# Dividing the 544 tokens of a matmul panel at another column: 272+272, 288+256, 512+32 and 364+180 in the four feed-forward stages of a decoder step

## The reference

```
x = x + 0.5 * swiglu(rms_norm(x, ffn1_norm), w_gate, w_up, w_down)
x = x + mixer(rms_norm(x, mix_norm))
x = x + 0.5 * swiglu(rms_norm(x, ffn2_norm), w_gate, w_up, w_down)
```

## Time and profile before

| what | value |
|---|---|
| time, median of 2 runs | 2168.56 us (2167.45 to 2169.67) |
| profiled execution, first to last instruction (its span) | 2169.2 us |
| PE busy | 2121.6 us, 98% of the span |
| PEld busy | 2040.0 us, 94% |
| DVE busy | 1028.8 us, 47% |
| ACT busy | 690.9 us, 32% |
| POOL busy | 274.7 us, 13% |
| TensorE clock granted, mean | 0.990 of full |
| HBM | 218.65 MB moved, 101 GB/s |

### The profile page before, as it was taken

One profiled execution on the slowest core, in us unless ns is written; L12 is line 12 of the kernel. 1 busy time (PEld: TensorE's weight loads), 2 busy tenths in 40 slices (PEclk: granted clock), 3 DMA queues, 4 the chain that ended last, 5 costly groups with the idle time before them and its releaser, 6 DMA issues.

```text
span 2169.2 us, 41417 instructions
## 1 busy us (share of the span) xinstructions
PE 2121.6 (98%) x16662; PEld 2040.0 (94%) x16662; DVE 1028.8 (47%) x1300; ACT 690.9 (32%) x908; POOL 274.7 (13%) x290
## 2 busy tenths in 40 slices
PE   9999999999999999999999999999988899999997
PEld 8999999997999999999999999999844799999997
DVE  6442444567654324455442444656835364424443
ACT  5221222237254212224441222222334244412221
POOL 0000111300310000021000001403145320000012
PEclk9999999999999999999999999999999999999999
DMA  3222432222132222222222222322589322222221
GB/s 143 87 96 79 131 108 94 91 69 73 69 107 89 91 83 88 89 93 71 86 102 83 78 90 96 112 91 83 153 236 267 117 85 87 102 82 78 87 100 68
DMA packets 68710, 218.65 MB, mean 101 GB/s; under 512 B 10186, under 2 KB 22645, under 8 KB 68544
## 3 DMA queue, kind: packets, MB, share of 16 engines
q1 hardware_dynamic: 58864, 191.00, 26.2%
q0 software_dynamic: 9184, 24.80, 4.1%
q10 hardware_dynamic: 576, 1.67, 0.2%
HBM read 212.67 MB, written 5.78 MB: 101 GB/s over the span
## 4 chain that ended last, share of the span: by engine, by line
PE 92%; DVE 3%; ACT 1%; DMA 1%; issue 1%; SPq 1%; DVEq 0%; ACTq 0%
PE ps L646 87%; PE ps L1067 1%; DVE rinv L1543 1%; DMA keys<-pool_kt 1%; DVE w_lo L1533 1%; PE ps L1094 1%; SPq L523 0%; PE ps L999 0%; ACT prob L1311 0%; DMA x<-xT 0%; PE ps L974 0%; PE ps L665 0%; PE ps L949 0%; PE ps L986 0%; PE ps L960 0%
## 5 line engine op out<-in xcount | busy, mean ns | idle before, releaser
L1210 ACT ACTIVATE w_hi<-raw 128x1024 fp32r<-128x1024 f32 (+2 forms) x298 | 334.8, 1124 | 1181.4 <-PE ps L646 1173.4
L646 PE MATMUL ps<-hx_hi,w_hi 128*128 128x272 f32 x3376 | 702.6, 289 | 5.1 <-DVE w_lo L1533 2.9
L646 PE MATMUL ps<-hx_hi,w_lo 128*128 128x272 f32 x3376 | 699.5, 289 | 0.0
L646 PE MATMUL ps<-hx_lo,w_hi 128*128 128x272 f32 x3376 | 696.9, 288 | 0.0
L646 PEld LDWEIGHTS ps<-hx_hi,w_hi 128*128 128x128 f32 x3376 | 531.8, 188 | 9.9 <-issue 5.8
L646 PEld LDWEIGHTS ps<-hx_lo,w_hi 128*128 128x128 f32 x3376 | 531.5, 189 | 0.0
L646 PEld LDWEIGHTS ps<-hx_hi,w_lo 128*128 128x128 f32 x3376 | 527.8, 189 | 0.0
L1533 DVE TENSOR_TENSOR w_lo<-raw,w_hi 128x1024 fp32r<-128x1024 f32 (+2 forms) x298 | 421.1, 1413 | 97.0 <-ACT w_hi L1210 96.7
L646 PE MATMUL ps<-hid_hi,w_hi 128*128 128x272 f32 x1408 | 291.1, 288 | 0.0
L646 PE MATMUL ps<-hid_lo,w_hi 128*128 128x272 f32 x1408 | 290.9, 288 | 0.0
L646 PE MATMUL ps<-hid_hi,w_lo 128*128 128x272 f32 x1408 | 290.8, 288 | 0.0
(11 more groups left out here) (315 smaller groups left out, 1516.5 us busy)
## 6 DMA issues: line engine op xcount, KB each, us to landing
raw<-gu SPq DMA_DIRECT2D x175, 512.0 KB, 3.2
raw<-down SPq DMA_DIRECT2D x64, 704.0 KB, 4.0
keys<-pool_kt SPq DMA_DIRECT2D x128, 144.0 KB, 4.5
vals<-pool_v POOLq DMA_DIRECT2D x128, 128.0 KB, 4.7
raw<-odd_in SPq DMA_DIRECT2D x21, 512.0 KB, 3.2
raw<-even_in SPq DMA_DIRECT2D x14, 512.0 KB, 3.2
raw<-even_out SPq DMA_DIRECT2D x8, 512.0 KB, 3.2
raw<-odd_out SPq DMA_DIRECT2D x8, 512.0 KB, 3.9
```

Source lines behind the costliest of these rows:

```text
L646: last = pe.matmul(acc[slot][0:m, a, 0:TH], w, r[:, t, a * TH:(a + 1) * TH], start=(begin and t == tiles[0] and one == 0), stop=((end if s ...
L1210: act.activation(w_hi[slot][:, 0:cols], raw[slot][:, 0:cols], ACT.Copy).then_inc(w_hi_done, 1)
```

## The change

The cut column becomes a parameter of the stage. The two matmuls of a product take columns 0 to split - 1 and split to 543. The accumulator is now one run of 544 columns, placed so that its column `split` is the first of the second bank; each matmul still writes in one bank. The stages f0 to f3 get the splits 272, 288, 512 and 364; the mixers keep 272.

```
+SPLIT = 272
+FFN_SPLIT = (272, 288, 512, 364)
...
-        def acc_of(slot, rows=P):
-            return acc[slot][0:rows, :, 0:TH]
+        def acc_of(slot, rows=P, split=SPLIT):
+            at0 = 2 * slot * BANK + BANK - split
+            return ps_flat[rows if isinstance(rows, slice) else slice(0, rows), at0:at0 + T]
...
-                    for w, r, one in ((hi, rhs_hi, 0), (hi, rhs_lo, 1), (lo, rhs_hi, 2)):
-                        for a in token_halves:
-                            last = pe.matmul(acc[slot][0:m, a, 0:TH], w, r[:, t, a * TH:(a + 1) * TH],
...
+                    for a in token_halves:
+                        c0, c1 = (0, split) if a == 0 else (split, T)
+                        out = acc_of(slot, m, split)[:, c0:c1]
+                        pe.matmul(out, hi, rhs[:, 0, t, c0:c1], start=opens, stop=False)
+                    for a in token_halves:
+                        c0, c1 = (0, split) if a == 0 else (split, T)
+                        pe.matmul(acc_of(slot, m, split)[:, c0:c1], hi, rhs[:, 1, t, c0:c1], start=False, stop=False)
+                    for a in token_halves:
+                        c0, c1 = (0, split) if a == 0 else (split, T)
+                        last = pe.matmul(acc_of(slot, m, split)[:, c0:c1], lo, rhs[:, 0, t, c0:c1], start=False, stop=closes)
```

The readers of the accumulator take one run of 544 columns in place of two of 272 (BANK is 512):

```
-                        dve.tensor_tensor(halves(gate[:]), acc_of(n0 % 2), halves(rinv[:]), ALU.mult).then_inc(acc_read, 1)
+                        dve.tensor_tensor(gate[:], acc_of(n0 % 2, split=split), rinv[:], ALU.mult).then_inc(acc_read, 1)
...
-                dve.scalar_tensor_tensor(out=xm, in0=acc_of(slot), scalar=factor, in1=xm, op0=ALU.mult, op1=ALU.add)\
+                dve.scalar_tensor_tensor(out=xm, in0=acc_of(slot, split=split), scalar=factor, in1=xm, op0=ALU.mult, op1=ALU.add)\
```

More of the change, by code:

```diff
@@ L153, in decoder_step @@
         put = region(region_hid, end_hid)
-        mix_hi = put("mix_hi", [P, DT, T], F32R)
-        mix_lo = put("mix_lo", [P, DT, T], F32R)
+        mix = put("mix", [P, 2, DT, T], F32R)
+        mix_hi, mix_lo = mix[:, 0], mix[:, 1]
+        mix_base = [region_hid + s * size([P, DT, T]) for s in range(2)]
         spare = region_hid + 2 * size([P, DT, T])
@@ L288, in decoder_step @@
         ps_flat = ps[:].rearrange("p b c -> p (b c)")
-        acc = [ps[:, 2 * s:2 * s + 2, :] for s in range(2)]
+        BANK = 512
         def sem(name):
@@ L631, in _, with panel @@
         def _(pe):
-            def panel(n, slot, rhs_hi, rhs_lo, tiles, wait_input=None, m=P, begin=True, end=True, token_halves=(0, 1), stop=None, first=False):
+            def panel(n, slot, rhs, tiles, wait_input=None, m=P, begin=True, end=True, token_halves=(0, 1), stop=None, first=False, split=SPLIT):
                 if begin:
@@ L643, in panel @@
                     hi, lo = w_hi[slot][:, t * m:(t + 1) * m], w_lo[slot][:, t * m:(t + 1) * m]
[L644 to L648 removed]
+                    opens = begin and t == tiles[0]
+                    closes = (end if stop is None else stop) and t == tiles[-1]
+                    for a in token_halves:
[8 more added lines that the diff above has]
+                        last = pe.matmul(acc_of(slot, m, split)[:, c0:c1], lo, rhs[:, 0, t, c0:c1], start=False, stop=closes)
                 if end:
@@ L672, in ffn @@
             def ffn(start, f, norm):
+                how = dict(split=FFN_SPLIT[f])
                 for c in range(CHUNKS):
@@ L696, in ffn @@
                         for s in range(2):
-                            panel(n0 + 2 * i + s, (n0 + s) % 2, hx_hi, hx_lo, range(DT))
+                            panel(n0 + 2 * i + s, (n0 + s) % 2, hx, range(DT), **how)
                     if f == 0 and c == 0:
@@ L713, in mixer_out_begin @@
                 for t in which:
-                    panel(start + t, (start + t) % 2, mix_hi, mix_lo, tiles, end=False)
+                    panel(start + t, (start + t) % 2, mix, tiles, end=False)
             def mixer_out(start, early, late, pieces, token_halves=(0, 1)):
@@ L719, in mixer_out @@
                 for t in range(2):
-                    panel(start + t, (start + t) % 2, mix_hi, mix_lo, late, begin=False, token_halves=token_halves)
+                    panel(start + t, (start + t) % 2, mix, late, begin=False, token_halves=token_halves)
                 for t in range(2, DT):
-                    panel(start + t, (start + t) % 2, mix_hi, mix_lo, early + late)
+                    panel(start + t, (start + t) % 2, mix, early + late)
             def by_distance():
@@ L897, in even @@
                     if k < 0:
-                        panel(n, n % 2, hx_hi, hx_lo, range(DT), split_input if t == 0 else None)
+                        panel(n, n % 2, hx, range(DT), split_input if t == 0 else None)
                     else:
-                        panel(n, n % 2, hx_hi, hx_lo, range(DT // 2), end=False)
+                        panel(n, n % 2, hx, range(DT // 2), end=False)
                         unit_score(k)
@@ L903, in even @@
                             unit_values(k - 2)
-                        panel(n, n % 2, hx_hi, hx_lo, range(DT // 2, DT), begin=False)
+                        panel(n, n % 2, hx, range(DT // 2, DT), begin=False)
                         if k >= 1:
@@ L1108, in out_begin @@
                 pe.wait_ge(mix_done, MLA_PIECE + HEADS)
[L1109 to L1110 removed]
+                panel(n, n % 2, mix, CONV_TILES, end=False)
+                panel(n, n % 2, mix, MLA_TILES, begin=False, end=False, token_halves=(0,), stop=True)
             def attend():
@@ L1164, in split_cq @@
                         pe.wait_ge(cq_done, t + 1)
-                    panel(n, n % 2, cq_hi, cq_lo, range(QT), split_cq if h == 0 else None)
+                    panel(n, n % 2, cq, range(QT), split_cq if h == 0 else None)
                     if h == 0:
@@ L1548, in scaled @@
                 dve.wait_ge(panel_done, n + 1)
-                dve.tensor_tensor(halves(out), acc_of(n % 2, rows), halves(by), ALU.mult).then_inc(acc_read, 1)
+                dve.tensor_tensor(out, acc_of(n % 2, rows), by, ALU.mult).then_inc(acc_read, 1)
             def input_lo(norm, m):
@@ L1604, in ffn @@
             def ffn(start, f, norm):
+                split = FFN_SPLIT[f]
                 for c in range(CHUNKS):
```

66 lines of the change are left out of this document (33 added, 33 removed).

## The result

| kernel | median us | ratio to before, 95% interval |
|---|---|---|
| before | 2168.56 (2 runs) | |
| changed | 2357.25 (2355.45 to 2359.05, 2 runs) | 1.0877 [1.084, 1.0914] |

The changed kernel is 8.8% slower, 189 us. The forecast was 2350 us, with 2295 to 2400.

A forecast was written before the change was run, and what follows sets the result against it. PE's matmul starts were taken to bound the feed-forward stages. Terms 143 (f2) + 40 (f3) + 0 (f1, readers) - 1 (waits) = +182 us on the median 2168.56 gave 2350 us, range 2295 to 2400.

The forecast's parts named there:

- The narrow part, 110 ns: Narrow matmul of a product: below some 110 ns it is charged 110, read from 128-wide weight loads for 32-column matmuls.
- The wide part, 231 ns: f2's 512-column matmul: scaled to 225 or 236 ns, 231 taken as the middle, bound from below 213.
- the 12 ns: Excess of a 272-column matmul, 125.3 ns, over one column a cycle, 113.3; either fixed per matmul or growing with columns.
- f2, 143 us: f2 at 512 + 32: a product takes 231 + 110 = 341 ns, 90 more, times 1584 = 143 us.
- f3, 40 us: f3 at 364 + 180: a product takes 166 + 110 = 276 ns, 25 more, times 1584 = 40 us.
- f1, 0 us: f1 at 288 + 256: both parts exceed 110 ns, so the product stays 250.6; cost 0, 11 us at most.
- The waits, -1 us: Start of f2 and f3: the slower first panel covers the weight split, some 0.5 us of wait gone in each, together -1.
- A load of 125 ns: Rival, all feed-forward matmuls: the weight load itself takes 125 ns and sets today's pace; about 2399 to 2410 us; chance 18%.
- Nothing is lost: Rival, split products: the narrow matmul hides its successor's load, so only columns and excess count; 2169 us; chance 5%.
- its case with 59 ns: In-between rival: a load costs 59 ns, from a row with 64-wide weights; f2 +62, f3 nothing, about 2230 us; chance 3%.
- width is almost free: Rival: issue sets the pace, a wide matmul takes 125 ns and a narrow one 110; 2119 us, faster; chance 1%.
- The clock falls: Rival, f2: PE drops to 1.2 GHz as the array works less of each product; some 2836 us; chance 2%.

The follow-up runs named there:

- the grouped run: Changed kernel with splits 272, 280, 512, 256; in f2 alone a tile's three wide matmuls come first, then its three narrow ones: 2317.29 us.
- the three-stage run: Changed code at 272+272 everywhere; f1 matmuls each open and close their sum, f2 operands read as bfloat16, f3 weights 64 columns wide: 2150.7 us.

## Why the prediction was right

**The bound.** That the distances between PE's starts set the time in the stages, and nothing else would appear, held: 145.7 + 40.6 of 184.6 us are distances between PE's starts, and DVE, ACT and SP show no new wait in f2 or f3.

**The narrow part, 110 ns.** Right in size, and shown by taking it away: half the weights of the wide matmul take off 53 ns, half those of the narrow one 3. The traces show it directly in two ways: 108.8 ns between the two loads of a product in f2, and 111 to 112 ns between starts in the grouped run. So 110 was sized within 2 ns. The choice of rows 8 over rows 9 was right, but the prediction's reading of rows 9, "half the weights and about half the time", was luck: that row stood at a granted clock of 0.53, and rows 8 at 1.00. The same 32 matmuls in the changed kernel, at 1.00, take 1.17 us and not 1.90, and start 29 ns apart:

```profile
1853.83 1.17 PE ps L1157 x32
```

So the 59 ns are no price at full clock, and the chance of the case built on them rested on a misread row. And these plain float32 loads of 64 columns follow faster than the 55 ns of the feed-forward type. Why is open.

**The wide part, 231 ns.** Right within a few ns: 231.6 between starts in the grouped run, 235.6 between loads in f2 of the changed kernel, and 344.2 less 109 to 112 for the narrow part gives 232 to 235. That lies between the two ways in which the 12 ns could go, 225 and 236, and nearer to the second. The excess over one column a cycle is 12 ns at 272 columns and 18 to 22 at 512 (213.3 to 231.6 and 235.6): it grows with the columns, if perhaps not quite in proportion.

**f2, 143 us.** 1584 x (344.2 - 250.6) = 148 us. Between the statistics it shows as 145.7, since the first panel of f2, 24 x 94 ns = 2 us, lies in f1's stretch and a wait of 0.5 us went at its start. The 5 us missing are 1584 times the 3 ns between a product of 341 and one of 344.

**f3, 40 us.** 1584 x (277.5 - 251) = 42 us; between the statistics, without the first panel, it shows as 40.6. Both parts right: 166 was thought for 364 columns, and 277.5 less 109 to 112 leaves 166 to 169.

**f1, 0 us.** Its gate and up panels gained 2.8 ns a product, 1056 x 2.8 = 3 us, and its down panels nothing (251.5 for 251.7). The stretch shows only -0.8, for the dearer first panel of f2 lies in it. The term was thought 0 up to +11; the sign was off. It is the smallest of the terms.

**The readers, 0.** 725 ns before and after, and the ratio 0.9999 with even halves.

**The waits, -1 us.** Right: before, PE waited 0.54 us for `w_lo` behind the first two panels of f2 and of f3, and in the changed kernel both waits are gone. The line of the earlier trace rows, 5.1 us in 7 waits, reads after the change:

```profile
PE ps L653 <- DVE w_lo L1545: 4.3, 5, 1.3
```

In the time it can't be seen apart: stretches of one kernel differ by 0.8 us from run to run and those in the mixers by 2 to 4.

**What I said the profile would show.** The starts were to alternate at 231 and 110 ns. They alternate at 317 and 28. The sum is right, the reading of a start was wrong: the record of a matmul's start does not say that its columns stream. The wide one is recorded as started 28 ns after the narrow one, while its weights are being loaded until some 109 ns; then come its 232 to 236 ns. The prediction had named "the narrow matmul's successor starts within 60 ns" as a sign that it is wrong. By the recorded starts this sign came, and it was a bad sign: taken alone, the 28 ns would have spoken for the rival in which nothing is lost. What decides is the distance over a whole product, and the distance between the loads.

**The rivals.** *A load of 125 ns*: 304 + 240 at 252 and not 265 speaks against it, and half weights in f3 of the three-stage run change 1 ns. *Nothing is lost*, its case with 59 ns, and *width is almost free*: ruled out by the time itself. *The clock falls*: 1.00 through f2.

## What to carry to other kernels

In this stream a matmul is charged the longer of its own columns and the load of the weights behind it: 0.46 ns a streamed column against 0.83 ns a weight column, so with 128-wide weights each matmul wants some 240 columns or more. The price of a load is shown for this type and for 64 and 128 columns; the plain float32 row above, 29 ns with 64-wide weights, doesn't follow it, so measure it for another type. Cut a token dimension that doesn't fit in one bank into parts that all clear this bound, rather than into one full bank and a rest; near the even cut there is a flat range, in which some 16 columns more or less can be worth half a per cent, so try them. Judge such a stream by the distance over a whole product and not by single starts.

## What the runs showed of the hardware

- Loads of weights are repeated even when the next matmul has the same weights: three narrow matmuls in a row, the first two with the same `w_hi`, take 112 ns each (grouped run).
- A matmul's start is recorded before its weights are in: 28 ns behind the narrow one, when by the 109 ns between the loads some 80 ns of load are to go (an estimate).
- Float32 operands of this type stream at 0.45 to 0.46 ns a column at a granted clock of 1.00, 0.44 when read as bfloat16 at the same addresses, and at 0.83 at half clock, which is one a cycle there. What takes the last 7 ns of 272 columns at full clock is open; leaving out the accumulation changed nothing, and half the weight columns at most 1 ns.
- 288 + 256 takes 247.8 ns where 272 + 272 takes 250.6 and 280 + 264 254.3, with 8 tiles a panel; with 11 tiles the three take 251.5, 250.1 or 251.7, and 250.7. The single distances repeat in a fixed pattern through a stage. In f1 the mean distance with DVE busy and with DVE idle is 250.3 and 250.7 ns before and 246.9 and 248.5 with 288 everywhere, so the other engines aren't seen to slow it, though no run rules them out. The cause was not found.
